# Attention in a two-layer hybrid backbone: the transposes of the values stand directly beside those of the row sums, two score tiles later

## The chip, the cores and the metric

One core of a Trainium2 chip runs the whole program. The metric is device time in microseconds of one execution. A core has five engines with instruction streams of their own: TensorE (PE in the profile, its weight loads PEld), VectorE (DVE), ScalarE (ACT), GpSimd (POOL) and SyncE (SP, which issues transfers). They meet through semaphores alone, and each runs its own stream in the order in which it is written.

## What is computed

Two layers of a backbone, for 1024 latent tokens (8 tiles of 128) and 128 prompt tokens (the ninth tile). Each layer projects its input, runs grouped-query attention, an mLSTM and a gated MLP side by side, projects back and ends with a feed-forward part. The change is in the attention. Eight query heads share two key and value heads (four query heads to each); the latent queries see 128 cached keys and the 1024 latent ones, nine tiles of keys; the prompt's queries see the prompt's own tile.

```python
def blocked_attention(q, k, v):
    B, T = q.shape[0], q.shape[1]
    nb = T // Q_BLOCK
    qb = q.reshape(B, nb, Q_BLOCK, ATT_KV_HEADS, ATT_GROUP, HEAD_DIM).transpose(1, 0, 2, 3, 4, 5)
    scale = HEAD_DIM ** -0.5

    def one_block(qblk):
        s = jnp.einsum('bqkgd,bskd->bkgqs', qblk, k).astype(jnp.float32) * scale
        p = jax.nn.softmax(s, axis=-1).astype(v.dtype)
        return jnp.einsum('bkgqs,bskd->bqkgd', p, v)

    o = lax.map(one_block, qb)
    return o.transpose(1, 0, 2, 3, 4, 5).reshape(B, T, ATT_WIDTH)
```

## The kernel before

The attention of a layer is a walk over 18 steps: nine query tiles (`t`), and in each the two key and value heads (`g`). A step works on 4 query heads of 128 queries. It is a pipeline over three steps that are in flight at once, written out by hand in the function `step` of TensorE's stream (line 2251), with a `step` of its own in the streams of ScalarE, VectorE and GpSimd. `nk`, `pk` and `nn` are the numbers of key tiles of this step, of the one before and of the next one (9 for latent queries, 1 for the prompt's). For the step at hand `j` runs over the key tiles, and in each turn TensorE issues, in this order:

- `scores_T` (lines 2189, 2190): the transposed scores of all four heads against key tile `j`, two products into bank 3 or 4. ScalarE takes their exponential (line 1038) into `pr`. The product of tile `j` waits until the exponential of tile `j - 2` is out.
- at `j` 1, the first work of other steps: `scores` of head 0 of the next step, then the last of the products with the values of the step before, `pairs`, `ninth` and `row_sums` (all through line 2199): weighted values in bank 5, row sums in bank 6.
- `outputs_T` and `sums_T` for the step before: ScalarE copies bank 5 to `o_s` (line 1049) and bank 6 to `sm_s` (line 1054) at its own tile 1; TensorE turns each by four transposes of 128x128, `o_s` into bank 7 (line 2242) and `sm_s` into bank 6 (line 2248). The last transpose of `sums_T` gives the semaphore `ot_ps`, on which VectorE starts `outputs` (lines 1625 to 1632), that divides the values by the sums.
- `scores` of heads 1, 2 and 3 of the next step at `j` 1, 3 and 6, as `SCORES_AT = {1: 1, 3: 2, 6: 3}` says (lines 2169, 2171): scores of one head against all nine key tiles, into banks 0 to 2, for the row maximum alone. VectorE takes that maximum (line 1610, `mx_done`), and the scores of the next head wait for it, because they go into the same banks. Between its maxima VectorE normalises and rotates the queries of the step after the next (lines 1549 to 1571).
- at `j` 6, `pairs` for the first three pairs of tiles of this step (line 2199), and then `shift` (line 2195): one product that spreads the row maxima of the next step from a diagonal which GpSimd has made (line 742). ScalarE copies its result to `q_lo` (line 1043).
- at the end `queries_T` (line 2157): the transposes of the queries of the step after the next.

What sets the order around the change is only this text: TensorE runs it as it stands. A call to `outputs_T` waits for `o_cp` (the copy of bank 5), and, when a next step exists, for `q_lo_done`, since bank 7 holds the turned queries until VectorE has read them. `sums_T` waits for `sm_cp`. After the walk, lines 2316 to 2321 do the same for the last step, with `outputs_T` and `sums_T` one directly behind the other.

Of the kernel before, what the change touches and what calls it, by code (L numbers as in the profile page):

```python
# [195 lines left out]
def build(nc, x_in, cond, w_mod, m_slots, b_mod, b_cols, w_slots, consts, rope, cache_k, cache_v, state0, row_in,  # L196
# [6 lines left out]
    with ExitStack() as ctx:  # L203
# [268 lines left out]
        def counts(L, t, g):  # L472

            if isinstance(t, int) and t == NS:
                return (NG * L + 2 * NS + g, N_E * L + 2 * NS * NT + g, N_P * L + 2 * NS * PASSES,
                        N_A * L + 2 * NS * 3)
            return (NG * L + 2 * t + g, N_E * L + 2 * NT * t + NT * g, N_P * L + 2 * PASSES * t + PASSES * g,
                    N_A * L + 6 * t + 3 * g)
# [1428 lines left out]
        def _(pe):  # L1907
# [56 lines left out]
            for L in range(NL):  # L1964
# [187 lines left out]
                def queries_T(G, g):  # L2152

                    pe.wait_ge(S["qd_done"], G + 1)
                    pe.wait_ge(S["oy_done"], START + G - 2)
                    for h in range(HG):
                        mm = pe.transpose(ps[:, 7, h * P:(h + 1) * P], qd[:, g * HG + h].rearrange("p a b -> p (a b)"), ident[:])
                    mm.then_inc(S["q_ps"], 1)

                def scores(G, g, h, nk, pk, bank=0):  # L2160


                    pe.wait_ge(S["mx_done"], START + HG * G + h - (1 if bank or not pk and G % NG == 0 else 0))
                    if h == 0:
                        pe.wait_ge(S["q_hi_done"], G + 1)
                    tiles = kst[:, g, 0:NS * P].rearrange("p (a b c) -> p a b c", b=2, c=P)
                    for b in range(2):
                        a = key_rows(b)
                        pe.matmul(ps[:, bank + b, :], q_hi[a, g, h], tiles[a, :, b], start=True, stop=True)  # L2169
                    a = key_rows(NS)  # L2170
                    pe.matmul(ps[:, bank + 2, 0:P], q_hi[a, g, h], kst[a, g, NS * P:NT * P], start=True, stop=True).then_inc(S["s_ps"], 1)  # L2171

                def scores_last(G, g):

                    pe.wait_ge(S["mx_done"], START + HG * G)
                    pe.wait_ge(S["q_hi_done"], G + 1)
                    for h in range(HG):
                        mm = pe.matmul(ps[:, 0, h * P:(h + 1) * P], q_hi[:, g, h], kst[:, g, NT * P:(NT + 1) * P], start=True, stop=True)
                    mm.then_inc(S["s_ps"], HG)

                def scores_T(G, E, g, j, nk, pk):

                    if j == 0:
                        pe.wait_ge(S["q_lo_done"], START + G + 1)
                        pe.wait_ge(S["mb_done"], G + 1)
                    pe.wait_ge(S["ex_done"], START + E + j - 1)
                    k2 = slice((j if nk == NT else NT) * P, (j + 1 if nk == NT else NT + 1) * P)
                    out = ps[:, 3 + (j + g) % 2, :]
                    pe.matmul(out, kst[:, g, k2], q_hi[:, g].rearrange("p a b -> p (a b)"), start=True, stop=False)  # L2189
                    pe.matmul(out, kst2[:, g, k2], q_lo[:, g].rearrange("p a b -> p (a b)"), start=False, stop=True).then_inc(S["st_ps"], 1)  # L2190

                def shift(G, g):

                    pe.wait_ge(S["dg_done"], HG * G + HG)
                    pe.matmul(ps[:, 0, :], one_r[:], dg[:, g].rearrange("p a b -> p (a b)"), start=True, stop=True).then_inc(S["mb_ps"], 1)
# [5 lines left out]
                def pairs(G, E, g, i):  # L2201

                    if i == 0:
                        pe.wait_ge(S["o_cp"], START + G)
                    pe.wait_ge(S["ex_done"], START + E + 2 * i + 2)
                    side(0, HD, 5, vst[:, g, 2 * i], pr[:, 2 * i], i == 0, False)
                    side(HD, HD, 5, vst[:, g, 2 * i + 1], pr[:, 2 * i + 1], i == 0, i == 3).then_inc(S["pv_done"], 1)

                def ninth(G, E, g):

                    pe.wait_ge(S["ex_done"], START + E + NT)
                    pe.wait_ge(S["oy_done"], START + G)
                    side(0, 32, 5, vst[:, g, 8, 0:32], pr[:, 8], False, True)
                    side(32, 32, 5, vst[:, g, 8, 32:HD], pr[:, 8], False, True)
                    side(64, 32, 6, ones[:, 0:32], pr[:, 7], True, False)
                    side(96, 32, 6, ones[:, 0:32], pr[:, 8], True, False).then_inc(S["pv_done"], 1)

                def row_sums(A, g):

                    pe.wait_ge(S["sum_done"], START + A + 3)  # L2220
                    side(0, 32, 6, ones[:, 0:32], psm[:, g], True, True)
                    side(32, 32, 6, ones[:, 0:32], pr[:, 4], True, True)
                    side(64, 32, 6, ones[:, 0:32], pr[:, 5], False, True)
                    side(96, 32, 6, ones[:, 0:32], pr[:, 6], False, True).then_inc(S["pv_done"], 1)
# [13 lines left out]
                def outputs_T(G):  # L2238

                    pe.wait_ge(S["o_cp"], START + G + 1)  # L2240
                    for h in range(HG):
                        pe.transpose(ps[:, 7, h * P:(h + 1) * P], o_s[:, h * P:(h + 1) * P], ident[:])

                def sums_T(G, n=1):

                    pe.wait_ge(S["sm_cp"], START + G + 1)
                    for h in range(HG):
                        mm = pe.transpose(ps[:, 6, h * P:(h + 1) * P], sm_s[:, h * P:(h + 1) * P], ident[:])
                    mm.then_inc(S["ot_ps"], n)

                def step(t, g, nk, pk, nn, prep):
                    G, E, B, A = counts(L, t, g)
                    e1, a1 = E - pk, A - (3 if pk > 1 else 0)
                    for j in range(nk):
                        scores_T(G, E, g, j, nk, pk)
                        if not pk and j == 1:
                            queries_T(G + 1, 1 - g)
                        if nn and j == min(1, nk - 1):
                            if nn > 1:
                                scores(G + 1, 1 - g, 0, nn, pk)  # L2260
                            else:
                                scores_last(G + 1, 1 - g)
                        if pk > 1 and j == min(1, nk - 1):
                            pairs(G - 1, e1, 1 - g, 3)
                            ninth(G - 1, e1, 1 - g)
                            row_sums(a1, 1 - g)
                        if pk > 1 and j == min(3, nk - 1):
                            if nn:
                                pe.wait_ge(S["q_lo_done"], START + G + 2)
                            outputs_T(G - 1)  # L2270
                        if pk > 1 and j == min(5, nk - 1):
                            sums_T(G - 1)
                        for key, h in SCORES_AT.items():
                            if nn > 1 and j == min(key, nk - 1):
                                scores(G + 1, 1 - g, h, nn, pk)
                        if nk > 1 and j == 6:
                            for i in range(3):
                                pairs(G, E, g, i)
                        if nn and j == max(nk - 3, 0):
                            shift(G + 1, 1 - g)  # L2280
                    if nn and prep is not None:
                        queries_T(G + 2, g)
# [13 lines left out]
                pe.wait_ge(S["k_ones"], L + 1)  # L2296
                pe.wait_ge(S["v_st"], L + 1)
                walk(pe, L, step)
                def y_turned(t):

# [198 lines left out]
```

## Time and profile before

| | |
|---|---|
| median of 3 executions | 3110.93 us (3108.32 to 3113.79) |
| span of the profiled execution | 3114.3 us, mean granted TensorE clock 0.980 |
| busy in that span | TensorE 2989.0 us, VectorE 1929.1, ScalarE 995.1, GpSimd 403.8 |
| instructions | 43652 |

The attention walks lie at about 403 to 650 us and 1936 to 2183 us of the span. The views used below: the page gives busy times of whole engines; the sums by stretch give the same for a part of the span, with the granted clock; the timeline lists instructions by start, merged when they repeat; the view of one line gives all its instructions and what its engine waited for in front of them. "PE" durations are those of a pipelined unit whose ends are modelled, so the distance between two starts tells what an instruction costs.

### The profile page before, as it was taken

The page shows a single profiled execution, that of the slowest core. Times are in us where ns is not written, and L with a number is a line of the kernel's source. Part 1 is how long each engine was busy: PE and PEld are TensorE (multiplying, and loading weights), DVE is VectorE, ACT ScalarE, POOL GpSimd, SP SyncE. Part 2 cuts the span into 40 slices and gives each one's busy share as a digit, 9 for nine tenths or more (in the row PEclk, how much of TensorE's full clock was granted, in tenths as well). Part 3 has the DMA queues.
Part 4 walks back from the last instruction along what each step waited for, and adds up shares of the span by engine and source line. Part 5 has one row for each costly group of instructions (what it writes and reads, how often), then busy time and mean ns, then how long its engine had stood idle before and what let it go on. Part 6 is the DMA issues. An engine that isn't in the chain of part 4 may idle for free.

```text
span 3114.3 us, 43652 instructions
## 1 busy us (share of the span) xinstructions
PE 2989.0 (96%) x16207; PEld 2463.1 (79%) x16207; DVE 1929.1 (62%) x3490; ACT 995.1 (32%) x1948; POOL 403.8 (13%) x582
## 2 busy tenths in 40 slices
PE   6999989999999999999979998999999999999998
PEld 5787844567899899988968887454788999889997
DVE  4547777745776677766575577777467444554447
ACT  3322345535221222211353233445261221212212
POOL 1012333411000000000020033433010000000002
PEclk8999989999999999999989999999999999999999
DMA  7331210012132223322121111100212010111102
GB/s 290 122 124 42 72 62 0 0 50 69 63 109 63 73 82 108 95 68 91 33 99 56 33 52 60 61 0 27 72 41 68 28 55 28 55 41 41 54 28 75
DMA packets 93846, 201.45 MB, mean 65 GB/s; under 512 B 12432, under 2 KB 13088, under 8 KB 93024
## 3 DMA queue, kind: packets, MB, share of 16 engines
q1 hardware_dynamic: 78240, 151.76, 15.0%
q0 software_dynamic: 15424, 47.25, 4.4%
q8 instruction: 116, 1.90, 0.3%
q14 instruction: 66, 0.54, 0.1%
HBM read 181.88 MB, written 17.08 MB: 64 GB/s over the span
## 4 chain that ended last, share of the span: by engine, by line
PE 56%; issue 29%; DVE 7%; DVEq 2%; DMA 2%; ACT 1%; POOL 1%; POOLq 1%; SPq 0%; ACTq 0%
PE ps L1947 12%; PE ps L1951 12%; PE ps L1950 12%; PE ps L2199 6%; PE ps L2189 3%; PE ps L2190 2%; PE ps L2169 2%; DMA w_raw<-in_w_slots 1%; PE ps L2078 1%; DMA modw<-in_w_mod 1%; DVE xr L1736 1%; DVEq L1735 1%; DVE w_lo L532 1%; PE ps L1929 1%; PE ps L2035 1%
## 5 line engine op out<-in xcount | busy, mean ns | idle before, releaser
L1947 PE MATMUL ps<-hi,w_hi 128*128 128x384 f32 x1536 | 515.1, 335 | 4.0 <-DVE w_lo L532 4.0
L1951 PE MATMUL ps<-hi,w_lo 128*128 128x384 f32 x1536 | 513.4, 334 | 0.0
L1950 PE MATMUL ps<-lo,w_hi 128*128 128x384 f32 x1536 | 513.2, 334 | 0.0
L527 ACT CAST w_hi<-w_raw 128x512 fp32r<-128x512 f32 x368 | 215.0, 619 | 758.2 <-PE ps L1947 676.7
L1947 PE MATMUL ps<-w_hi,hi 128*128 128x512 f32 (+1 forms) x1008 | 394.2, 391 | 12.7 <-ACT stg L865 5.5
L1950 PE MATMUL ps<-w_lo,hi 128*128 128x512 f32 (+1 forms) x1008 | 384.1, 381 | 0.0
L1951 PE MATMUL ps<-w_hi,lo 128*128 128x512 f32 (+1 forms) x1008 | 383.9, 381 | 0.0
L1776 DVE TENSOR_TENSOR ps<-ps,gate 128x512 f32<-128x512 f32 x288 | 201.0, 698 | 238.2 <-PE ps L1951 238.1
L1947 PE MATMUL ps<-w_hi,f_hi 128*128 128x512 f32 x864 | 337.4, 391 | 8.3 <-DVE xr L1779 4.3
L1951 PE MATMUL ps<-w_hi,f_lo 128*128 128x512 f32 x864 | 336.9, 390 | 0.0
L1950 PE MATMUL ps<-w_lo,f_hi 128*128 128x512 f32 x864 | 336.9, 390 | 0.0
L532 DVE TENSOR_TENSOR w_lo<-w_raw,w_hi 128x512 fp32r<-128x512 f32 x368 | 239.1, 690 | 103.0 <-ACT w_hi L527 100.6
L1947 PEld LDWEIGHTS ps<-hi,w_hi 128*128 128x128 f32 x1536 | 288.3, 188 | 8.3 <-DVE w_lo L532 3.4
L1950 PEld LDWEIGHTS ps<-lo,w_hi 128*128 128x128 f32 x1536 | 288.3, 188 | 0.5
L1951 PEld LDWEIGHTS ps<-hi,w_lo 128*128 128x128 f32 x1536 | 288.3, 188 | 0.0
L1763 DVE TENSOR_TENSOR f_sq<-f_sq 128x384 f32<-128x384 f32 x144 | 80.1, 556 | 248.8 <-ACT f_hi L1112 248.3
L1947 PEld LDWEIGHTS ps<-w_hi,hi 128*128 128x128 f32 x1008 | 193.9, 192 | 49.5 <-DVE w_lo L532 5.9
L1951 PEld LDWEIGHTS ps<-w_hi,lo 128*128 128x128 f32 x1008 | 193.7, 192 | 36.0
L1950 PEld LDWEIGHTS ps<-w_lo,hi 128*128 128x128 f32 x1008 | 194.1, 193 | 31.6
L1110 ACT ACTIVATE f_sq<-ps 128x384 f32<-128x384 f32 x144 | 70.8, 492 | 420.2 <-PE ps L1951 420.2
L1947 PEld LDWEIGHTS ps<-w_hi,f_hi 128*128 128x128 f32 x864 | 162.5, 188 | 42.8 <-DVE xr L1779 5.2
L1610 DVE TENSOR_REDUCE nm<-ps 128x1 f32<-128x1152 f32 x128 | 173.2, 1354 | 34.1 <-PE ps L2171 33.4
(319 smaller groups left out, 4805.8 us busy)
## 6 DMA issues: line engine op xcount, KB each, us to landing
w_raw<-in_w_slots SPq DMA_DIRECT2D x368, 256.0 KB, 3.2
w_raw<-in_m_slots SPq DMA_DIRECT2D x160, 256.0 KB, 3.0
out<-xr POOLq DMA_DIRECT2D x18, 512.0 KB, 3.2
modw<-in_w_mod SPq DMA_DIRECT2D x4, 2048.0 KB, 15.5
acc<-in_x_in SPq DMA_DIRECT2D x3, 1536.0 KB, 16.2
zq_dram<-stg POOLq DMA_DIRECT2D x18, 256.0 KB, 2.3
xr<-in_x_in POOLq DMA_DIRECT2D x2, 2304.0 KB, 10.6
xr<-out POOLq DMA_DIRECT2D x2, 2304.0 KB, 10.7
```

The lines of the kernel that those rows point to most:

```text
L527: act.copy(w_hi[:, j, :], w_raw[:, j % RAW, :]).then_inc(S["w_hi_done"], 1)
L532: dve.tensor_tensor(w_lo[:, j, :], w_raw[:, j % RAW, :], w_hi[:, j, :].bitcast(F32), ALU.subtract).then_inc(S["w_lo_done"], 1)
L1110: act.activation(f, ps[:, b % 3, 0:GRP].rearrange("p (a b) -> p a b", b=P), ACT.Relu).then_inc(S["r_done"], 1)
L1610: dve.tensor_reduce(nm[:, g, h:h + 1], i_, AX.XY, ALU.max, negate=True).then_inc(S["mx_done"], 1)
L1763: dve.tensor_tensor(f, f, f, ALU.mult)
L1776: dve.tensor_tensor(f, f, gate2[:, int(t < NS), h_ * W:(h_ + 1) * W], ALU.mult)
L1947: mm = pe.matmul(out, a_hi, b_hi, start=first, stop=False)
L1950: pe.matmul(out, a_hi, b_lo, start=False, stop=False)
L1951: return pe.matmul(out, a_lo, b_hi, start=False, stop=last)
L2169: pe.matmul(ps[:, bank + b, :], q_hi[a, g, h], tiles[a, :, b], start=True, stop=True)
L2189: pe.matmul(out, kst[:, g, k2], q_hi[:, g].rearrange("p a b -> p (a b)"), start=True, stop=False)
L2199: return pe.matmul(ps[j:j + w, bank, :], weights, moving, start=start, stop=stop)
```

## The change

The values' transposes (with the wait that guards bank 7) leave key tile 3 and stand in front of the sums' transposes at key tile 5. Nothing else differs: neither the other engines' streams nor any semaphore's count.

```diff
--- before.py
+++ after.py
@@ -2264,11 +2264,10 @@
                             pairs(G - 1, e1, 1 - g, 3)
                             ninth(G - 1, e1, 1 - g)
                             row_sums(a1, 1 - g)
-                        if pk > 1 and j == min(3, nk - 1):
+                        if pk > 1 and j == min(5, nk - 1):
                             if nn:
                                 pe.wait_ge(S["q_lo_done"], START + G + 2)
                             outputs_T(G - 1)
-                        if pk > 1 and j == min(5, nk - 1):
                             sums_T(G - 1)
                         for key, h in SCORES_AT.items():
                             if nn > 1 and j == min(key, nk - 1):
```

## Rows read from the trace of the kernel before

**Rows 1.** The page: busy us (share of the span) x instructions of each engine.
```profile
PE 2989.0 (96%) x16207; PEld 2463.1 (79%) x16207; DVE 1929.1 (62%) x3490; ACT 995.1 (32%) x1948; POOL 403.8 (13%) x582
```
**Rows 2.** Sums by stretch: stretch, length, busy us (x instructions) by engine, PEclk, DMA, GB/s.
```profile
440.00:630.00 190.00, 189.51 (x1007) 95.80 (x1010) 145.26 (x226) 98.51 (x180) 75.06 (x93) 1.00 0.02 6
648.90:652.10 3.20, 2.04 (x20) 1.73 (x16) 1.05 (x6) 1.66 (x3) 0.00 (x0) 1.00 0.00 0
```
**Rows 3.** Timeline of TensorE, one step: start us, us, engine, line, op, out<-in, count.
```profile
475.57 0.40 PE L2189 MATMUL ps<-q_hi,kst 128*128 128x512 f32 x1
475.81 0.39 PE L2190 MATMUL ps<-q_lo,kst 128*128 128x512 f32 x1
476.03 0.60 PE L2242 MATMUL ps<-ident,o_s 128*128 128x128 f32 x4
476.69 0.50 PE L2169 MATMUL ps<-kst,q_hi 64*128 64x512 f32 x2
...
478.21 0.60 PE L2248 MATMUL ps<-ident,sm_s 128*128 128x128 f32 x4
478.59 0.50 PE L2189 MATMUL ps<-q_hi,kst 128*128 128x512 f32 x1
478.93 0.40 PE L2190 MATMUL ps<-q_lo,kst 128*128 128x512 f32 x1
479.25 0.51 PE L2169 MATMUL ps<-kst,q_hi 64*128 64x512 f32 x2
...
482.46 0.50 PE L2195 MATMUL ps<-dg,one_r 128*128 128x512 f32 x1
```
**Rows 4.** Timeline of VectorE, the second head's maximum in the same step.
```profile
475.29 1.35 DVE L1610 TENSOR_REDUCE nm<-ps 128x1 f32<-128x1152 f32 x1
```
**Rows 5.** Timeline of TensorE in the step before, around the third head's scores.
```profile
461.28 0.39 PE L2190 MATMUL ps<-q_lo,kst 128*128 128x512 f32 x1
...
462.04 0.49 PE L2169 MATMUL ps<-kst,q_hi 64*128 64x512 f32 x2
```
**Rows 6.** Timeline of VectorE in the step before, the second head's maximum.
```profile
460.59 1.36 DVE L1610 TENSOR_REDUCE nm<-ps 128x1 f32<-128x1152 f32 x1
```
**Rows 7.** View of line 2169, 440 to 620 us: what ended idle time, us, times.
```profile
  DVE nm L1610: 2.8, 13
```
**Rows 8.** View of line 2242, whole span: duration ns min/median/max, first and last start.
```profile
L2242 PE MATMUL ps<-ident,o_s x136: 270/272/300, 433.2 to 2182.8; 128*128 128x128 f32 x136
```
**Rows 9.** Timeline of TensorE at the end of layer 0's walk.
```profile
649.90 0.60 PE L2242 MATMUL ps<-ident,o_s 128*128 128x128 f32 x4
650.34 0.60 PE L2248 MATMUL ps<-ident,sm_s 128*128 128x128 f32 x4
```
**Rows 10.** Timelines of GpSimd and VectorE, the last diagonal and the start of `outputs`.
```profile
481.53 0.40 POOL L742 TENSOR_TENSOR dg<-ident,nm 128x128 fp32r<-128x128 f32 x1 [1.50 <-DVE nm L1610]
481.62 0.17 DVE L1625 TENSOR_REDUCE rinv<-ps 128x4 f32<-128x16 f32 x1 [0.17 <-issue]
```
**Rows 11.** Timelines of ScalarE and TensorE behind `shift`, to the next step's first product.
```profile
483.61 1.09 ACT L1038 ACTIVATE pr<-ps 128x512 f32<-128x512 f32 x2
483.73 0.60 PE L2157 MATMUL ps<-ident,qd 128*128 128x128 f32 x4
484.26 0.50 PE L2189 MATMUL ps<-q_hi,kst 128*128 128x512 f32 x1
```
**Rows 12.** Timeline of TensorE in the first step of layer 0; [idle before <-releaser].
```profile
412.70 0.80 PE L2169 MATMUL ps<-kst,q_hi 64*128 64x512 f32 x2 [4.63 <-DVE nm L1610]
...
414.55 0.63 PE L2189 MATMUL ps<-q_hi,kst 128*128 128x512 f32 x1
414.97 0.63 PE L2190 MATMUL ps<-q_lo,kst 128*128 128x512 f32 x1
```
**Rows 13.** Timeline of TensorE, the `shift` of the step after that of rows 3.
```profile
496.56 0.50 PE L2195 MATMUL ps<-dg,one_r 128*128 128x512 f32 x1
```
**Rows 14.** View of line 1610, whole span: duration ns min/median/max, first and last start.
```profile
L1610 DVE TENSOR_REDUCE nm<-ps x128: 1344/1357/1359, 396.1 to 2154.3; 128x1 f32<-128x1152 f32 x128
```

## What I expect of the time, and why

> **What bounds the kernel now.** I read the page first: TensorE is busy for 96% of the span, VectorE for 62% [rows 1]. Then the sums by stretch: in the attention loop of layer 0, from 440 to 630 us, TensorE is busy for 189.51 of 190 us at a granted clock of 1.00, with VectorE at 145, ScalarE at 99 and GpSimd at 75 us [rows 2]. So TensorE is the bound there, and anything that lets it wait is paid for unless the wait is there already. The busy time is no proof of that, since the modelled ends of matmuls overlap (a product of 0.39 us is followed by the next after 0.23), so from here on I read starts, not durations.
>
> The timeline of one attention step shows how close the other engines stand. TensorE's order between the products of key tile 3 and those of tile 4 is: four transposes of the values (L2242) at 476.03, then the scores of the third head (L2169) at 476.69 [rows 3]. Those scores go into banks 0 to 2, the ones from which VectorE takes the maximum of the head before (L1610), and `scores` waits for it. VectorE starts that maximum at 475.29 and takes 1.35 us, so it ends at 476.64 [rows 4], and the scores start 0.05 us behind it. In the step before it the same pair stands at 462.04 [rows 5] against an end at 460.59 + 1.36 = 461.95 [rows 6]: 0.09 us apart. The four transposes fill almost exactly the time that VectorE needs. I looked at all 28 steps in which scores follow: in 16 the distance is 0.09 to 0.10 us, in 12 it is 0.05, and the maximum ends at the same place each time. The loader of weights confirms the releaser: in 440 to 620 us, 13 of its waits in front of L2169, one for each step, end with VectorE's maximum [rows 7].
>
> **What changes, part by part.** The transposes are 136, four for each of 34 calls [rows 8]. Of the 17 calls in a layer, one stands behind the walk and one in the step of a single key tile, where 3, 5 and 0 are the same place; 15 move. Of these, 14 have scores of the third head behind key tile 3, and one (the last step of nine tiles, which prepares the one-tile query block) has none.
>
> 1. Taken away at tile 3, in 28 steps. Without the transposes the scores would follow the last product at the distance that a product and scores have elsewhere, 478.93 to 479.25 = 0.32 us [rows 3], so they would be ready at 475.81 + 0.32 = 476.13 in place of 476.69, and at 461.28 + 0.32 = 461.60 in place of 462.04 [rows 5]. But they can't start before the maximum is out. The closest that they come to it is the 0.05 us of the 12 tight steps, so they start at 476.69 as before, and at 461.95 + 0.05 = 462.00. The time saved is nothing in 12 steps and 0.04 us in 16: 16 x 0.04 = 0.6 us. What was work becomes idle time, 0.56 us in the one kind of step and 0.40 in the other. The scores of the second head, from which this maximum starts, stand in front of all of it and don't move, nor does anything that VectorE has queued ahead, so the maximum comes no earlier.
>
> 2. Added at tile 5, in 28 steps. The nearest row is the end of the layer, where the same two groups already stand one behind the other: L2242 at 649.90, L2248 at 650.34 [rows 9]. Four more transposes in front of L2248 cost 0.44 us. Bounds: not below the 0.38 us from the first of the sums' transposes to the next product [rows 3], and not above the 0.48 that come out when that product's slower start behind transposes is put in too (0.34 us to its partner, 478.59 to 478.93, against 0.24 at 475.57 to 475.81) [rows 3]. That slower start is paid today by L2248 alone and stays one, so I take 0.44. 28 x 0.44 = 12.3 us. The Trainium skill, page "TensorE: Matmul & The Clock Gate", section "Back-to-back issue gap", gives about 81 ns for a matmul of 128 columns in a sustained stream with its weight load, and its section "LDWEIGHTS (loading the stationary operand)" gives columns / 1.2, or 107 ns, for the load. By the first the added group would be 0.32 us and the whole change about 8 us; by the second 0.43 and the sum stays; the row's 0.44 over four decides for the second.
>
> 3. The two steps without scores. There the transposes stand between products at both places. One slower start (0.34 in place of 0.24 us) goes: 2 x 0.1 = 0.2 us saved.
>
> 4. The waits that move. `q_lo_done` guards bank 7; VectorE fulfils it at the start of a step. `o_cp` and `sm_cp` are given near tile 1. Neither is late at tile 5, so no price. The semaphore on which VectorE waits for the finished transposes is given by `sums_T`, which goes back by the 0.44 us. VectorE reaches that work only at 481.62, behind its fourth maximum [rows 10], and the sums' transposes end at 478.21 + 0.60 = 478.81 today [rows 3]; 0.44 more stays 2.4 us ahead. No DMA and no queue of SP or GpSimd is passed.
>
> 5. What would be late next. Everything of TensorE from tile 6 on shifts by 0.40 to 0.44 us: scores of the fourth head, twelve products with the values, then `shift` at 482.46 [rows 3]. Does that last one wait for others already, so that the delay could vanish? GpSimd's last diagonal ends at 481.53 + 0.40 = 481.93 [rows 10], 0.53 us ahead of `shift`. It does not. Behind `shift` TensorE does wait, for ScalarE (the exponentials of the last two tiles), but this chain starts from `shift`: the copy of the row maximum, then L1038 at 483.61, then the next step's product at 484.26 [rows 11]. The whole chain moves along, and the next step begins later by the full amount. Nothing outside the attention loop touches this.
>
> Sum: 12.3 - 0.6 - 0.2 = 11.5 us. Against the profiled span that is 3114.3 + 11.5 = 3125.8. The three timed executions lie at 3108.3 to 3113.8 with a median of 3110.93, 3.4 us below the profiled one, so the forecast of the median is 3110.93 + 11.5 = **3122.4 us**, 0.37% slower. A measurement of this kernel can tell about 0.2%, 6.2 us, from no change.
>
> **The rivals.** A. *Given back behind `shift`.* Were the tail of a step bound by something that doesn't hang on TensorE, the delay would be eaten there. The room is the wait of the next step's first product: 483.73 to 484.26 = 0.53 us [rows 11] where transposes and the product behind them take 0.38 [rows 3], so 0.15 us in this step; for the steps that begin a turn of the loop, which are some 0.2 us longer, I allow 0.25. That is about 28 x 0.2 = 5.6 us. That gives 11.5 - 5.6 = 5.9 us, 3116.8, just within 0.2%. Against it stands the chain of point 5.
>
> B. *The wait isn't the maximum's.* This is the rival on the other side. If the scores came when they do only because the transposes end there, they would move up by 0.44 us (0.56 in the tight steps) at each removal. The two groups cost the same 0.44 wherever they stand, so 16 steps would come out even and 12 would win 0.12, and with the 0.2 of point 3 the kernel would be 1.6 us faster: 3109.3. It decides as soon as the maximum of the second head ends more than 0.4 us before the third head's scores start. For it: the loader's waits are short, 2.8 us for 13 [rows 7]. Against it: the end of the maximum and the start of the scores are tied to 0.05 us in 12 steps whose other distances differ, which chance doesn't do. A version of this that gains more would need a shorter maximum with no transposes writing beside it; but the 128 maxima of the whole kernel take 1.344 to 1.359 us, whatever TensorE does beside them [rows 14].
>
> C. *The clock falls.* Each step gets an idle stretch of 0.4 to 0.56 us and a run of eight transposes. In the first step of the layer the scores came behind 4.63 us of idle time, and products then stand 0.42 us apart [rows 12] in place of 0.24, the level of 1.2 GHz. A step takes 14.10 us from one `shift` to the next [rows 3, 13], so one at that level, 1.75 times as long, costs 14.1 x 0.75 = 10.6 us more; one in each layer would give 3122.4 + 21 = 3144. Against it: from 648.9 to 652.1 us TensorE did nothing but sixteen transposes and a pause, and its granted clock was 1.00 [rows 2].
>
> **How the numbers follow.** Forecast 0.82, A 0.06, B 0.06, C 0.03, something else 0.03. The terms alone give from 28 x 0.38 - 0.8 = 9.8 to 28 x 0.48 - 0.2 = 13.2 us, 3120.7 to 3124.1. To this I add what separates medians of three (the spread was 5.5 us) and A at the lower end: 3115 to 3128. Faster by over 0.2% needs more than B offers: 0.03. Within 0.2% come B, A and a disturbed measurement: 0.13. Slower: 0.84.
>
> **What would show it.** The timeline of the changed kernel should have L2169 of the third head at 0.05 us behind the end of L1610 in every step, with an idle time of 0.40 to 0.56 us in front of it that VectorE ends (right: point 1; if it starts earlier, B). The values' transposes should stand 0.44 us in front of the sums' (point 2). The distance from one `shift` to the next should grow by 0.44 us in the tight steps and by 0.40 in the others, in the one from 482.46 from 14.10 to 14.50 (if less, A). The granted clock of the loop should read 1.00 (if not, C). The prediction is wrong if the period grows by less than 0.3 us.

## The result: 0.36% slower, and the profile after

| | median | range | executions |
|---|---|---|---|
| before | 3111.99 us | 3108.32 to 3114.34 | 8 |
| changed | 3123.36 us | 3115.00 to 3127.13 | 8 |

The ratio is 1.0036 with a 95% interval of 1.0027 to 1.0045, that is 8.4 to 14.0 us. The span of the profiled execution is 3125.3 us, 11.0 more than before.

The medians scatter by more than the effects that are looked for here, but the traces scatter less: inside the attention walks of the kernel before a step has the same length in both layers to 0.02 us, or to 0.06 where it begins a turn of the loop (the first such turn of a layer differs by 0.17). So I give beside each ratio how long both walks are, from the second `shift` (L2195) of a layer to its last. The first step of a layer is left out, since it waits for other things and varies by a microsecond and more. The view of line 2195, with the first and the last start in each layer, before:

```profile
L2195 PE MATMUL ps<-dg,one_r x17: 474/504/504, 425.3 to 644.3; 128*128 128x512 f32 x17
L2195 PE MATMUL ps<-dg,one_r x17: 474/504/504, 1958.0 to 2176.9; 128*128 128x512 f32 x17
```

and after the change:

```profile
L2195 PE MATMUL ps<-dg,one_r x17: 475/499/504, 426.8 to 650.5; 128*128 128x512 f32 x17
L2195 PE MATMUL ps<-dg,one_r x17: 474/499/505, 1962.5 to 2186.1; 128*128 128x512 f32 x17
```

At two digits the starts give 218.96 and 218.88 us before, 223.74 and 223.60 after: **+4.78 and +4.72, together 9.5 us**. The other 1.5 us of the spans' difference lie outside these stretches, in code that the change doesn't touch; the stretch between the two walks is anything from 5 us shorter to 2 us longer in the kernels of this study.

The sums by stretch answer to [rows 2]: length, then busy us (and instructions) of TensorE, its weight loader, VectorE, ScalarE and GpSimd, then the granted clock. TensorE lost 4.6 us of busy time in the same 190 us, at the same granted clock of 1.00:

```profile
440.00:630.00 190.00, 184.94 (x983) 92.23 (x979) 141.48 (x221) 95.23 (x173) 73.63 (x92) 1.00 0.00 0
```

The timeline of TensorE in the step that answers to [rows 3]:

```profile
477.99 0.40 PE L2190 MATMUL ps<-q_lo,kst 128*128 128x512 f32 x1
478.86 0.50 PE L2169 MATMUL ps<-kst,q_hi 64*128 64x512 f32 x2 [0.48 <-DVE nm L1610]
...
480.38 0.60 PE L2242 MATMUL ps<-ident,o_s 128*128 128x128 f32 x4
480.81 0.60 PE L2248 MATMUL ps<-ident,sm_s 128*128 128x128 f32 x4
481.17 0.48 PE L2189 MATMUL ps<-q_hi,kst 128*128 128x512 f32 x1
481.48 0.40 PE L2190 MATMUL ps<-q_lo,kst 128*128 128x512 f32 x1
481.81 0.51 PE L2169 MATMUL ps<-kst,q_hi 64*128 64x512 f32 x2
...
485.02 0.50 PE L2195 MATMUL ps<-dg,one_r 128*128 128x512 f32 x1
```

and VectorE's second maximum in that step [rows 4]:

```profile
477.45 1.35 DVE L1610 TENSOR_REDUCE nm<-ps 128x1 f32<-128x1152 f32 x1
```

The maximum ends at 478.80 and the scores start at 478.86; in all 28 steps with scores the distance is 0.05 to 0.06 us, as the forecast said. From the last product of tile 3 to the scores it takes 0.87 us, as it took 0.88 with the transposes in between [rows 3]. The place of the transposes is now 0.48 us of idle time that VectorE ends. For 440 to 620 us the view of the waits gives the total, the number and the longest; there [rows 7] had 2.8 us in 13 waits of the loader (12 steps with scores fall into this stretch now, 13 did before):

```profile
PEld ps L2169 <- DVE nm L1610: 9.9, 12, 0.9
PE ps L2169 <- DVE nm L1610: 4.6, 12, 0.5
```

### The profile page after: what moved, and what is told of

Read it like the earlier page. It is cut to its first block, busy times and chain, and to the rows that moved or that the text cites. A ratio compares the mean times of both kernels' runs of the same rounds, so it can differ in the third digit from the quotient of the medians.

```text
span 3125.3 us, 43652 instructions
## 1 busy us (share of the span) xinstructions
PE 2990.7 (96%) x16207; PEld 2463.1 (79%) x16207; DVE 1929.1 (62%) x3490; ACT 994.9 (32%) x1948; POOL 402.9 (13%) x582
## 4 chain that ended last, share of the span: by engine, by line
PE 50%; issue 30%; DVE 9%; DVEq 3%; DMA 2%; ACT 2%; POOL 1%; POOLq 1%; SPq 0%; ACTq 0%
PE ps L1947 12%; PE ps L1950 12%; PE ps L1951 12%; PE ps L2199 4%; DVE nm L1610 2%; DVEq L1551 1%; PE ps L2189 1%; DMA w_raw<-in_w_slots 1%; PE ps L2169 1%; PE ps L2190 1%; PE ps L2078 1%; DMA modw<-in_w_mod 1%; DVE xr L1736 1%; DVEq L1735 1%; DVE w_lo L532 1%
```

## The experiments

Two theories stand against each other. **Cover**: at tile 3 TensorE has to wait for VectorE anyway, four transposes fit into that wait, and whatever stands elsewhere is paid. **Neighbours**: two groups of transposes side by side cost more than apart, wherever they stand. All edits are against the kernel before unless said otherwise.

### Both groups at tile 3

```diff
                             outputs_T(G - 1)
-                        if pk > 1 and j == min(5, nk - 1):
                             sums_T(G - 1)
```

> The two groups of transposes stand side by side at key tile 3, with nothing at tile 5. Theory of the cover (tile 3 has room for one group, behind the maximum of the second head; whatever exceeds it is paid): the group that comes to tile 3 costs 0.44 us there. At tile 5 the product of tile 6 starts 0.05 us behind the exponential of tile 4 today, so taking the group away there saves at most 0.03. 30 steps x about 0.42 gives 10 to 12 us more than before, 3122 to 3124 (1.0032 to 1.0040). Theory of the neighbours (side by side they cost more than apart, wherever they stand): the same number. A theory that only tile 5 is a bad place: no change from before.

Ratio 1.0031 (1.0020 to 1.0042); the walks are 5.21 and 5.23 us longer. TensorE's timeline in one step:

```profile
476.91 0.60 PE L2248 MATMUL ps<-ident,sm_s 128*128 128x128 f32 x4
477.44 0.51 PE L2169 MATMUL ps<-kst,q_hi 64*128 64x512 f32 x2
...
478.73 0.40 PE L2190 MATMUL ps<-q_lo,kst 128*128 128x512 f32 x1
479.34 0.51 PE L2189 MATMUL ps<-q_hi,kst 128*128 128x512 f32 x1 [0.22 <-ACT pr L1038]
```

The scores come straight behind the second group, with no wait: that group is paid in full. And at tile 5, where it is missing, idle time appears that an exponential of ScalarE ends. From the last product of tile 5 to the first of tile 6 it takes 0.61 us, exactly what it took with the sums' transposes between them (477.98, not shown, to 478.59 [rows 3]). The exponential of tile 4 ends 0.05 us ahead of that product. So **each of the two places has a wait that holds one group**: VectorE's maximum at tile 3, ScalarE's exponential of tile 4 at tile 5. The kernel before had one group in each.

### The two groups swapped

`sums_T` stands at tile 3 and `outputs_T` at tile 5, and the last transpose of `outputs_T` signals (the second argument is the count that a group gives to `ot_ps`; the definitions, changed for it, are left out here).

```diff
...
                         if pk > 1 and j == min(3, nk - 1):
-                            if nn:
-                                pe.wait_ge(S["q_lo_done"], START + G + 2)
-                            outputs_T(G - 1)
+                            sums_T(G - 1, 0)
                         if pk > 1 and j == min(5, nk - 1):
-                            sums_T(G - 1)
+                            if nn:
+                                pe.wait_ge(S["q_lo_done"], START + G + 2)
+                            outputs_T(G - 1, 1)
```

> The two groups change places: the row sums' transposes at tile 3, the values' at tile 5, where the last one now signals. Apart, and one in each place. Theory of the cover: nothing changes, within 1.5 us of before (0.9995 to 1.0005), since it matters how many transposes stand at tile 3, not which. Theory that the values' group must be early (for its bank or for who reads it): slower by some us.

Ratio 1.0000 (0.9991 to 1.0009). The walks are 0.58 and 0.35 us longer, and 0.44 of it lies in each layer's one-tile step, where both groups stand in the same place and the first of them now waits for the later of ScalarE's two copies (0.70 us of idle time that L1054 ends). The nine-tile steps are the same to 0.05 us, but for one of 0.18. In these steps it matters how many transposes stand at a place, and not which.

### The values at tile 4

```diff
-                        if pk > 1 and j == min(3, nk - 1):
+                        if pk > 1 and j == min(4, nk - 1):
                             if nn:
                                 pe.wait_ge(S["q_lo_done"], START + G + 2)
                             outputs_T(G - 1)
```

> The values' transposes at tile 4, the sums' at tile 5: apart, but none at tile 3. Theory of the cover: as slow as the changed kernel or 1 to 3 us slower still, because a second slower start of a product (0.10 us) comes in while scores of the third head wait all the same: before + 10 to 14 us (1.0032 to 1.0045). Theory of the neighbours: as before, since they no longer stand side by side.

Ratio 1.0024 (1.0015 to 1.0033), walks +4.79 and +4.77, which is the changed kernel's loss to 0.05 us. The ratio came out below the 1.0032 to 1.0045 that I had expected. The groups stand apart, and it costs the same: the theory of the neighbours has fallen. Nor was there the extra 0.10 us that I expected of a second slower start:

```profile
476.03 0.60 PE L2242 MATMUL ps<-ident,o_s 128*128 128x128 f32 x4
476.39 0.48 PE L2189 MATMUL ps<-q_hi,kst 128*128 128x512 f32 x1
476.70 0.39 PE L2190 MATMUL ps<-q_lo,kst 128*128 128x512 f32 x1
476.93 0.60 PE L2248 MATMUL ps<-ident,sm_s 128*128 128x128 f32 x4
```

Four transposes take 0.36 us to the next product, which then needs 0.31 to its partner in place of 0.23. Without them the product would start where they start, and its partner 0.23 later, so they cost 0.36 + 0.31 - 0.23 = 0.44: the same 0.44 as beside another group.

### The values twice, at tile 3 and at tile 5

```diff
                         if pk > 1 and j == min(5, nk - 1):
+                            if nk > 1:
+                                outputs_T(G - 1)
                             sums_T(G - 1)
```

> The values' transposes are issued twice, at tile 3 as before and again at tile 5 beside the sums': the changed kernel with four transposes more in each of 30 steps, which write the same values to the same place. Theory of the cover: the four at tile 3 stand in idle time, so the time is that of the changed kernel within 2 us: before + 9.5 to 12.5 us. If the idle time in the changed kernel isn't usable (the scores would start later behind work), it is 28 x 0.44 = 12 us more than that, before + 23.

The walks are +4.99 and +5.06 us, 0.55 us more than the changed kernel's in both layers together, though they hold 120 transposes more. So the idle time at tile 3 can be used, and is nearly free. The ratio, 1.0041 (1.0029 to 1.0054, 9.0 to 16.8 us), is too wide to say more; the median, 14 us up, is not explained by the walks. The profiled execution is 15.9 us longer than that of the kernel before, and 5.9 of it lie outside the two stretches, in code that this edit doesn't touch; that part stays open.

### Two of four transposes moved

`outputs_T` takes the heads whose transposes it issues (its changed definition is left out).

```diff
-                            outputs_T(G - 1)
+                            outputs_T(G - 1, range(0, 2))
                         if pk > 1 and j == min(5, nk - 1):
+                            outputs_T(G - 1, range(2, 4))
                             sums_T(G - 1)
```

> Two of the four transposes of the values stay at tile 3, two go to tile 5 beside those of the sums. Theory of the cover: each transpose that leaves leaves idle time behind and costs 0.11 us where it goes, so a step is longer by 2 x 0.11 - 0.05 = 0.17 us in the wide steps and 0.1 in the tight ones, half of what the changed kernel loses, 4 to 5 us over both walks (ratio 1.0013 to 1.0016). Theory of the neighbours: the full loss, 9 us.

Ratio 1.0010 (1.0001 to 1.0019), walks +1.77 and +1.66, together 3.4 us. The timeline shows the idle time at half its size:

```profile
477.50 0.38 PE L2242 MATMUL ps<-ident,o_s 128*128 128x128 f32 x2
478.15 0.50 PE L2169 MATMUL ps<-kst,q_hi 64*128 64x512 f32 x2 [0.26 <-DVE nm L1610]
```

The loss goes with the number of transposes that leave, but it is 36% of the changed kernel's and not half: I had expected 4 to 5 us. One reason shows in the timelines: the 0.05 us that is saved at tile 6 (below) is there in full with the first two transposes already.

### The maximum made short, before and changed

This takes VectorE's maximum over four of nine key tiles, once on the kernel before and once on the changed one. Both leave a part of the computation out.

```diff
-                    i_ = ps[:, bank:bank + 3, :].rearrange("p a b -> p (a b)")[:, 0:NT * P].unsqueeze(1) if nk == NT
+                    i_ = ps[:, bank:bank + 3, :].rearrange("p a b -> p (a b)")[:, 5 * P:NT * P].unsqueeze(1) if nk == NT
```

> The kernel before with VectorE's row maximum taken over four of the nine key tiles (512 of 1152 columns), so that each takes some 0.65 us in place of 1.36; this leaves a part of the computation out. Nothing waits for a maximum at tile 3 then. Theory of the cover: 5 to 9 us faster than before, since the first steps of each layer wait 6 us for maxima and every step some tenths. It is the base for the next kernel.

> The changed kernel with the same shortened maximum. Theory of the cover: without a maximum to wait for, the scores of the third head start 0.44 us earlier when the transposes leave tile 3, which pays for the 0.44 at tile 5: in each step that has scores the two kernels with short maxima differ by less than 0.05 us, and only the last nine-tile step of each layer is 0.4 longer; together 0 to 2 us. Theory of the neighbours, or any theory in which tile 5 is the cause: the difference stays 9 to 11 us.

These two runs decide. With a maximum of 0.69 us the kernel before is at 0.9970 (0.9960 to 0.9979) and the changed one at 0.9964 (0.9950 to 0.9977); in the walks they stand at -1.25 and -1.17, and at -1.57 and -1.47 us. (The medians fell by more, among other things because each layer's first step, which waits for maxima, is 3.3 to 4.1 us shorter.) **Without the wait at tile 3 the same change costs nothing and even wins 0.6 us.** Each nine-tile step with scores is 0.02 to 0.08 us shorter than in the kernel before with a short maximum, and the last one of each layer is 0.4 longer, as expected. That the sum is 0.6 us below nothing, where I had expected 0 to 2 above, is the saving at tile 6 that comes up below. The timeline of the changed kernel with the short maximum shows the scores 0.33 us behind the product, the distance that I had taken from [rows 3]:

```profile
483.64 0.40 PE L2190 MATMUL ps<-q_lo,kst 128*128 128x512 f32 x1
483.97 0.51 PE L2169 MATMUL ps<-kst,q_hi 64*128 64x512 f32 x2
...
485.49 0.60 PE L2242 MATMUL ps<-ident,o_s 128*128 128x128 f32 x4
485.93 0.60 PE L2248 MATMUL ps<-ident,sm_s 128*128 128x128 f32 x4
```

### The outputs freed earlier

In the changed kernel the steps that begin a further turn of the loop, five in each layer, grew by 0.23 to 0.30 us, but the first of these in each layer by 0.07 and 0.12; the other nine-tile steps with scores grew by 0.33 to 0.38. The timelines of TensorE behind `shift`, before and after, at the same turn:

```profile
497.85 0.60 PE L2157 MATMUL ps<-ident,qd 128*128 128x128 f32 x4
498.46 0.49 PE L2189 MATMUL ps<-q_hi,kst 128*128 128x512 f32 x1
```

```profile
500.74 0.60 PE L2157 MATMUL ps<-ident,qd 128*128 128x128 f32 x4
501.26 0.50 PE L2189 MATMUL ps<-q_hi,kst 128*128 128x512 f32 x1
```

0.61 us became 0.52. `queries_T` waits for bank 7, which VectorE frees with the last operation of `outputs` (L1632). Before, that stood at

```profile
497.21 0.42 DVE L1632 TENSOR_TENSOR zq<-zq,rinv 128x256 f32 x1
```

so it ended at 497.63, 0.22 us ahead of the transposes; the branch of the loop lies behind this wait. After the change it stands at

```profile
499.76 0.42 DVE L1632 TENSOR_TENSOR zq<-zq,rinv 128x256 f32 x1
```

and ends at 500.18, 0.56 us ahead: the transposes moved by 2.89 us, VectorE's release by 2.55. To test this, VectorE leaves out the last operation of `outputs`, the multiplication by the reciprocal sums, and frees the bank with the one before.

```diff
-                    dve.tensor_tensor(o3, o3, o4[:, :, 0:HD], ALU.add)
-                    dve.drain()
-                    dve.tensor_tensor(o3, o3, b2(rinv[:, 0], HD), ALU.mult).then_inc(S["oy_done"], 1)
+                    dve.tensor_tensor(o3, o3, o4[:, :, 0:HD], ALU.add).then_inc(S["oy_done"], 1)
```

> The kernel before, in which VectorE leaves out the last operation of each output (the multiplication by the reciprocal row sum), so that it frees bank 7 about 0.5 us earlier; the outputs are not divided. It tests why the changed kernel won back 0.10 us in the steps that begin a turn of the loop. Theory: TensorE's sequencer stands at the wait for that bank in front of the transposed queries and gets to the branch of the loop too late. Then the wait of the next step's first product shrinks in these steps from 0.61 to 0.52 us behind the queries' transposes, and the step from 14.30 to 14.20, with other steps unchanged. Rival: the branch costs what it costs, and what shrank in the changed kernel is something else: no change.

The turn that answers to the pair above (its lines are numbered two lower):

```profile
497.74 0.60 PE L2155 MATMUL ps<-ident,qd 128*128 128x128 f32 x4
498.27 0.50 PE L2187 MATMUL ps<-q_hi,kst 128*128 128x512 f32 x1
```

0.53 us, and the step is 14.20 in place of 14.30. All ten turns of the two layers lose 0.06 to 0.46 us, no other step moves by more than 0.03, and the walks are 0.73 and 0.67 us shorter, in the one trace that there is of this kernel. The cause is the late release of bank 7, as supposed: VectorE's next operation waits for ScalarE before and after the edit, so no other release moves. That it acts through the branch fits the place, but the run doesn't show the branch itself.

### Two attempts to do better, and the two together

The findings name three waits of TensorE that the kernel before still has: 0.1 us for the maximum in the tight steps, 0.1 for bank 7 at the turns, and 0.14 behind `shift` in every step. For the first, VectorE's rotation of the next queries went behind the second maximum:

```diff
-PREP = ((0, 1), (), (2,), ())
+PREP = ((0,), (1,), (2,), ())
```

> The kernel before, with VectorE's rotation of the next queries moved from in front of the second head's maximum to behind it. Theory of the cover: in the tight steps (12 of 28) the maximum starts as soon as its scores are out, 0.1 us earlier, and the third head's scores follow the transposes at 0.20 us from the last one, as in the wide steps, where it was 0.33. Both walks together are 1 to 2 us shorter, too little for the median. If VectorE's work is only pushed on to the third maximum, the fourth head's scores or the shift come later by the same, and nothing is won.

For the third, tile 7 went ahead of the last pair of products with the values:

```diff
                     for j in range(nk):
-                        scores_T(G, E, g, j, nk, pk)
+                        if j != 7:
+                            scores_T(G, E, g, j, nk, pk)
...
                             for i in range(3):
+                                if i == 2:
+                                    scores_T(G, E, g, 7, nk, pk)
                                 pairs(G, E, g, i)
...
-                        if nn and j == nk - 2:
+                        if nn and nk > 1 and j == nk - 1:
                             max_out(G + 1, 1 - g)
```

> The kernel before, with the scores of key tile 7 issued ahead of the last pair of products with the values instead of behind the shift, and ScalarE's exponential of that tile ahead of the copy of the row maxima. It uses the same idea in the other direction: behind the shift TensorE waits 0.14 us in every step (0.53 from the queries' transposes to the next product, where 0.38 would do) for a chain on ScalarE of copy and two exponentials; with one exponential taken out of it the wait should go. 30 steps x 0.14 less about 0.05 for breaking the row of pairs, and 0.1 in the steps that begin a turn of the loop if that wait goes too: 3 to 5 us faster than before (0.9984 to 0.999). Rival: the next bound, the copy of the queries behind the same exponential, takes its place and the step stays as it is.

> The two edits together, on the kernel before. If they remove different waits their gains add up: 4 to 7 us over both walks (0.9978 to 0.9987).

All three missed, and are slower, in the order above: 1.0069 (1.0054 to 1.0085), 1.0022 (1.0012 to 1.0031) and 1.0102 (1.0087 to 1.0117); the walks +8.70 and +8.57, +3.61 and +3.34, +12.39 and +12.31 us. The two losses add up.

With the rotation behind the maximum, the place at tile 3 came out as expected: the scores follow the transposes without a wait. But the fourth head's scores now wait 0.64 us. Timelines of TensorE, VectorE and GpSimd in one step:

```profile
479.63 0.40 PE L2190 MATMUL ps<-q_lo,kst 128*128 128x512 f32 x1
480.67 0.49 PE L2169 MATMUL ps<-kst,q_hi 64*128 64x512 f32 x2 [0.64 <-DVE nm L1610]
```

```profile
477.56 1.38 DVE L1564 TENSOR_TENSOR qd<-qn,z 128x128 f32<-128x128 f32 x1
```

```profile
477.45 1.33 POOL L751 TENSOR_TENSOR psm<-psm,pr 128x512 f32<-128x512 f32 x1 [2.57 <-ACT pr L1038]
```

The operation L1564 took 1.38 us; in the kernel before, where GpSimd is idle at that time, it takes

```profile
474.88 0.29 DVE L1564 TENSOR_TENSOR qd<-qn,z 128x128 f32<-128x128 f32 x1
```

The other steps agree: in 26 steps of the two walks one L1564 takes 1.37 or 1.38 us and ends 0.15 us behind a GpSimd addition (L751), where the kernel before has 52 of 0.28 to 0.29 us and none beside an addition. No run takes the addition away, so this cause is read from traces.

With tile 7 ahead, the wait behind `shift` went down as intended (0.53 to 0.45 in every second step), and `shift` itself came later. The timeline there:

```profile
485.45 0.50 PE L2189 MATMUL ps<-q_hi,kst 128*128 128x512 f32 x1
485.79 0.40 PE L2190 MATMUL ps<-q_lo,kst 128*128 128x512 f32 x1
486.11 1.08 PE L2199 MATMUL ps<-pr,vst 128*64 128x512 f32 x4
487.12 0.50 PE L2195 MATMUL ps<-dg,one_r 128*128 128x512 f32 x1
```

The six pair products and tile 7 take 1.87 + 0.66 + 1.01 = 3.54 us from the first pair to `shift` (483.58, 485.45, 486.11, 487.12), where the undivided row took 2.73 (479.74 to 482.46) and tile 7 behind it 0.47: 0.34 us for interrupting the row once, for which I had allowed 0.05. No kernel of this study is faster than the one before with the whole computation in it.

## Why the prediction was right, and where its sum was off

The forecast was 3122.4 us and the range 3115 to 3128; the median is 3123.4. The mechanism held. The size came out closer than its terms deserve: both walks grew by 9.5 us where my terms give 11.5, and the medians happen to differ by 11.4 with an interval from 8.4.

**Point 1, nothing is saved at tile 3.** Right, and shown from both sides: the changed kernel's scores are tied to the maximum (0.05 to 0.06 us behind it in all 28 steps), and with a short maximum the cost is gone. Four other kernels (the swap, tile 4, twice, half) agree with a wait that holds one group.

**Point 2, 0.44 us for four more transposes at tile 5.** Right for the transposes: 480.38 to 480.81 is 0.43. What I missed lies behind them. I read the 0.38 us from the sums' transposes to the next product and its 0.34 to its partner as the price of transposes. In truth the product of tile 6 was held by ScalarE's exponential of tile 4 as well, which ended when the transposes did. With more transposes in front it isn't held: 0.36 (481.17 - 480.81) and 0.31. So the 0.38 us that I gave as a lower bound held a wait, and was none. That gives back 0.05 us a step, in 28 steps 1.4 us, so the steps that I had put at 0.40 grew by 0.33 to 0.38.

**Point 3, 0.2 us saved in the two steps without scores.** Wrong in sign: each is 0.42 or 0.39 us longer. Without scores there is no wait for VectorE, and I took the place to be open. But the product of tile 4 then comes early enough to wait for ScalarE's exponential of tile 2. Before, exponential and transposes ended together. ScalarE's row, then TensorE's:

```profile
631.39 0.60 ACT L1038 ACTIVATE pr<-ps 128x512 f32<-128x512 f32 x1
```

```profile
631.65 0.60 PE L2242 MATMUL ps<-ident,o_s 128*128 128x128 f32 x4
632.04 0.50 PE L2189 MATMUL ps<-q_hi,kst 128*128 128x512 f32 x1
```

and after the change:

```profile
637.17 0.60 ACT L1038 ACTIVATE pr<-ps 128x512 f32<-128x512 f32 x1
```

```profile
637.21 0.39 PE L2190 MATMUL ps<-q_lo,kst 128*128 128x512 f32 x1
637.82 0.50 PE L2189 MATMUL ps<-q_hi,kst 128*128 128x512 f32 x1 [0.23 <-ACT pr L1038]
```

The product starts 0.05 us behind the exponential in both (631.99 to 632.04, 637.77 to 637.82). The step of my reasoning that failed is "which wait ends last here": I checked VectorE's and stopped. Two steps of +0.4 in place of -0.1 are 1.0 us more.

**Points 4 and 5, nothing behind tile 6 gives the delay back.** Right for the chain from `shift` over ScalarE: the step from 482.46, put at 14.50 us, is 14.45. Wrong for the turns of the loop: 8 times some 0.12 us, and about 0.3 in each of the two first ones. The ten steps that begin a turn are among the twelve tight ones, which were to grow most, by 0.44; they grew least, by 0.07 to 0.30, and so below the 0.3 that the prediction named as the sign of being wrong. Rival A named the place (the next step's first product) and its bound of 5.6 us, but not the mechanism. It is VectorE's release of bank 7, which doesn't hang on TensorE's late part, as the kernel with the outputs freed earlier shows. Point 4 looked at the release of finished transposes to VectorE, not at what VectorE gives back. The terms then read: 11.5, less 1.4, plus 1.0, less 8 x 0.12 and 2 x 0.3 for the turns, which is the 9.5 measured. The last two terms, 1.56 us, are read from the growth of these very steps, so that the sum closes is no test of them; the kernel that frees bank 7 earlier is one, and lost 1.47 us in the ten turns.

**The rivals.** B (the wait isn't the maximum's) is out: the idle time is there, VectorE ends it. C (the clock falls) is out: the granted clock of the loop stayed at 1.00, with an idle stretch (0.48 us in the step shown) and eight transposes in a row in every step. By the 107 ns per weight load of the Trainium skill's page "TensorE: Matmul & The Clock Gate", section "LDWEIGHTS (loading the stationary operand)", the eight transposes should by my estimate stand about 0.11 us apart each, and they do (0.43 for four); the 81 ns of its section "Back-to-back issue gap" don't hold for these.

## What to carry to other kernels

Before moving independent work off an engine that seems full, ask for the place that it leaves which semaphore the next instruction would wait for, and when each of them arrives: here each of the two fillers stood in a wait of nearly its own length, so taking it away freed almost nothing and putting it elsewhere cost nearly its full price. Ask it for every kind of step, with and without the neighbour that gives the first wait, because behind the wait that you found a second one may stand close by: ScalarE's exponential and the transposes beside it ended within 0.05 us of each other. And when medians scatter by as much as the effect, measure the period of a marker instruction inside the loop: here the period told 9.5 us from the forecast's 11.5, which the medians' interval of 8.4 to 14.0 could not.

## What the runs showed of the hardware

- An operation of VectorE with both inputs in SBUF was stretched from 0.29 to 1.38 us while GpSimd's 1.33 us addition of two SBUF tiles ran beside it, and ended (478.94) just behind it (478.78), in 26 steps alike; the rotation's later addition (L1569), which stands beside a GpSimd addition in the kernel before and takes 1.00 to 1.17 us there, took 0.67 us in this kernel, where nothing of GpSimd's additions ran beside it. By contrast the maxima, which read PSUM, kept their duration of 1.34 to 1.36 us [rows 14], with an addition beside them or not. The Trainium skill, page "SBUF — State Buffer", section "SBUF: two separate sides", calls the pair of ports that the two engines share an exclusive lock, held for a whole instruction; the trace agrees. Where an instruction stands on VectorE is thus also a choice of what GpSimd does at that time.
- Four transposes of 128x128 cost 0.44 us wherever they stand, beside another group or alone between products. Alone, 0.08 of it shows up as a slower start of the next product.
- Interrupting a row of products that use half of the array's columns each (128*64) with one pair of full products (128*128) cost 0.34 us more than the 0.47 of the pair itself.
- A semaphore that arrives just in time for an instruction can still cost time at the turn of a loop: bank 7 was free 0.22 us before the transposes that wait for it started; freed one operation earlier, the turns were 0.06 to 0.13 us shorter, and the first of each layer 0.46 and 0.28. Which instruction of the turn is late, no run shows.
